# PSUM of the attention stage divided anew in a decoder-layer kernel: logits in two single banks, turned weights in two 1024-column places

## The reference, cut to what matters

```python
score = jnp.where(admissible[None], score, -jnp.inf)
_, idx = lax.top_k(score, topk)                       # 256 keys of each query
logits = jnp.einsum('btngd,btknd->btngk', qg, k_sel) * (HEAD_DIM ** -0.5)
logits = logits + bias                                # T5 bias by distance
p = jax.nn.softmax(logits, axis=-1)
o = jnp.einsum('btngk,btknd->btngd', p, v_sel)
...
y = causal_depthwise_conv(u, conv_w) + conv_b         # width 31
yn = (y - mean(y)) * lax.rsqrt(var(y) + LN_EPS)       # over channels
```

## Time and profile before

| | |
|---|---|
| median of 3 runs | 1701.25 us (1700.36 to 1712.43) |
| span of the profiled execution | 1700.2 us |
| PE matmul busy | 1513.3 us (89%) |
| PE weight load busy | 1292.1 us (76%) |
| DVE busy | 1003.3 us (59%) |
| ACT busy | 697.9 us (41%) |
| POOL busy | 415.0 us (24%) |

### The profile page before, as it was taken

How to read it: one execution, slowest core, us unless ns; L and a number is a source line. 1 busy time by engine, 2 the same in 40 slices (tenths; PEclk the granted TensorE clock), 3 DMA queues, 4 the chain that set the end, 5 groups by cost and what they waited for, 6 DMA issues and landing times. The chain is left out here.

```text
span 1700.2 us, 28238 instructions
## 1 busy us (share of the span) xinstructions
PE 1513.3 (89%) x10647; PEld 1292.1 (76%) x10647; DVE 1003.3 (59%) x2123; ACT 697.9 (41%) x1238; POOL 415.0 (24%) x270
## 2 busy tenths in 40 slices
PE   5688989989998789999799999999999887569998
PEld 5686979978998769999577777776767665348886
DVE  3342998878988879888443444445455555333222
ACT  4354513253112352232225545556556654344331
POOL 2111224431115803222221001112222233043220
PEclk9999999999999999999879999999999999779999
DMA  7742365221357602224561513511111112295542
GB/s 237 219 107 50 68 92 119 67 75 54 84 161 222 157 22 72 70 75 125 163 156 36 115 37 79 113 35 34 39 45 50 58 61 77 81 231 162 173 149 93
DMA packets 183355, 172.71 MB, mean 102 GB/s; under 512 B 58956, under 2 KB 155348, under 8 KB 182700
## 3 DMA queue, kind: packets, MB, share of 16 engines
q1 hardware_dynamic: 176572, 152.91, 33.7%
q10 hardware_dynamic: 6136, 16.95, 3.4%
q0 software_dynamic: 512, 1.05, 0.2%
HBM read 109.35 MB, written 58.19 MB: 99 GB/s over the span
## 5 line engine op out<-in xcount | busy, mean ns | idle before, releaser
L845 PE MATMUL psum<-xh,wh 128*128 128x384 f32 (+1 forms) x1040 | 345.4, 332 | 23.1 <-ACT hst L782 11.5
L845 PE MATMUL psum<-xl,wh 128*128 128x384 f32 (+1 forms) x1040 | 341.6, 329 | 0.0
L845 PE MATMUL psum<-xh,wl 128*128 128x384 f32 (+1 forms) x1040 | 341.6, 328 | 0.0
L1436 ACT ACTIVATE pts<-psT 128x512 f32<-128x512 f32 (+1 forms) x302 | 167.1, 572 | 255.1 <-PE psT L1717 232.2
L845 PEld LDWEIGHTS psum<-xh,wh 128*128 128x128 f32 x1040 | 197.6, 190 | 26.4 <-ACT hst L782 15.2
L1606 DVE CUSTOM_DVE_ANT_0 L<-psU,mask 128x512 f32<-128x512 f32 (+3 forms) x260 | 143.5, 592 | 114.6 <-PE psU L1711 113.3
L1733 PE MATMUL psO<-pts,vs 128*64 128x128 f32 x2176 | 180.3, 287 | 27.2 <-ACT pts L1436 27.2
L845 PEld LDWEIGHTS psum<-xl,wh 128*128 128x128 f32 x1040 | 197.8, 190 | 0.0
L845 PEld LDWEIGHTS psum<-xh,wl 128*128 128x128 f32 x1040 | 197.5, 190 | 0.0
L995 DVE TENSOR_SCALAR_CACHE_REDUCE hit<-scores,T 128x1792 bf16<-128x1792 f32 (+8 forms) x120 | 184.6, 1538 | 11.7 <-issue 0.9
L693 POOL TENSOR_TENSOR wl<-uw,wh 128x1024 fp32r<-128x1024 f32 x44 | 121.5, 2762 | 276.8 <-ACT wh L730 276.8
(11 more groups left out here) (269 smaller groups left out, 2507.5 us busy)
## 6 DMA issues: line engine op xcount, KB each, us to landing
uw<-in_w_in SPq DMA_DIRECT2D x28, 512.0 KB
uw<-in_w_in SPq DMA_DIRECT2D x32, 256.0 KB
qt<-d_q SPq DMA_DIRECT2D x16, 512.0 KB, 4.0
xst<-in_x_prompt SPq DMA_DIRECT2D x15, 512.0 KB, 4.0
xr<-in_x_prompt SPq DMA_DIRECT2D x15, 512.0 KB, 4.4
out_y_prompt<-fin SPq DMA_DIRECT2D x15, 512.0 KB, 3.0
gate<-d_ga SPq DMA_DIRECT2D x17, 256.0 KB, 4.4
d_mix<-mix SPq DMA_DIRECT2D x17, 256.0 KB, 2.2
```

Source lines behind the costliest of these rows:

```text
L845: last = nc.tensor.matmul(u[:, 0:k * P], a[:, w % 2, cc, :], x[:, s0:s0 + k, cc, :], start=(cc == 0 and e == 0), stop=(cc == KC - 1 and e ...
L1436: A.activation(out, src, ACT.Copy).then_inc(act_pt, 1)
```

## The change: what it does, and the diff

PSUM is divided anew: `U` has two single banks (PE may be two pieces ahead of DVE, not four), `PT` has two places of 1024 columns, which are two banks each, and `OT` stays. A group has up to four key blocks of both sides (step 0: eight), made as even as can be by `groups`. ACT copies a group of up to 1024 columns with one instruction. `pts` goes from three places of 512 to two of 1024.

PE's order in a step changes: the next step's pieces are laid between the turns, two by two. A turn waits for the exponentials of its own side alone. ACT takes the next step's first exponential after the first copy where a step has more than two groups, the second after all copies; the copy of the spread reciprocals (`rb`) moves behind both. SBUF buffer `L` loses its pad of 128 columns a row; row 0 alone runs over, for step 0.

```diff
-    per = lambda p: 2 if p else 4
-    groups = lambda p: [(b, min(per(p), nblk(pairs[p][0]) - b)) for b in range(0, nblk(pairs[p][0]), per(p))]
+    per = lambda p: 4 if p else 8
+    def groups(p):
+        n = nblk(pairs[p][0])
+        g = -(-n // per(p))
+        ends = [-(-n * e // g) for e in range(g + 1)]
+        return [(b, e - b) for b, e in zip(ends, ends[1:])]
+    u_pieces = lambda p: [(side, a, k) for side in range(sides(p)) for a, k in bank_pieces(pairs[p][0])]
...
-        pts = sb("pts", [128, 3, 4 * P])
+        pts = sb("pts", [128, 2, 8 * P])
...
-        U = ctx.enter_context(nc.psum_tensor("psU", [128, 2, UNIT], f32))
-        PT = ctx.enter_context(nc.psum_tensor("psT", [128, 2, 512], f32))
+        U = ctx.enter_context(nc.psum_tensor("psU", [128, 2, 512], f32))
+        PT = ctx.enter_context(nc.psum_tensor("psT", [128, 2, 8 * P], f32))
...
-            exps(0)
+            exps(0, 0)
             for p, (i, j) in enumerate(pairs):
-                for b, k in groups(p):
+                for e, (b, k) in enumerate(groups(p)):
                     job = ("T", p, b, k)
                     n = t_no[job]
-                    act.wait_ge(pe_pv, NS + 1 + max(0, n - 2))
+                    act.wait_ge(pe_pv, NS + 1 + max(0, n - 1))
                     m = sides(p) * k * P
-                    evac(job, pts[:, n % 3, 0:m], PT[:, pt_no[job] % 2, 0:m])
+                    evac(job, pts[:, n % 2, 0:m], PT[:, pt_no[job] % 2, 0:m])
+                    if e == 0 and len(groups(p)) > 2 and p + 1 < NP_:
+                        exps(p + 1, 0)
+                if p + 1 < NP_:
+                    if len(groups(p)) <= 2:
+                        exps(p + 1, 0)
+                    exps(p + 1, 1)
...
-                    evac(("R", p), rb[:, n % 2].rearrange("p c t -> p (c t)"), PT[:, pt_no["R", p] % 2, :])
-                if p + 1 < NP_:
-                    if j == GRP - 1 and tile_no[i] >= 1:
-                        act.wait_ge(ri_ready, tile_no[i])
-                    exps(p + 1)
+                    evac(("R", p), rb[:, n % 2].rearrange("p c t -> p (c t)"), PT[:, pt_no["R", p] % 2, 0:4 * P])
...
-                    pe.wait_ge(dve_u, max(first_logits, n - 3))
+                    pe.wait_ge(dve_u, max(first_logits, n - 1))
...
             def transposes(p, b, k):
                 pt = take_pt(("T", p, b, k))
                 for side in range(sides(p)):
+                    if b == 0:
+                        pe.wait_ge(exp_done, sides_before(p) + side + 1)
...
             for p, (i, j) in enumerate(pairs):
-                if p + 1 < NP_:
-                    logits(p + 1)
-                pe.wait_ge(exp_done, sides_before(p + 1))
+                gs = groups(p)
+                more = len(u_pieces(p + 1)) if p + 1 < NP_ else 0
+                if more:
+                    logits(p + 1, 0, 2)
+                transposes(p, *gs[0])
+                if more > 2:
+                    logits(p + 1, 2, 4)
+                if len(gs) > 1:
+                    transposes(p, *gs[1])
+                if more > 4:
+                    logits(p + 1, 4, 6)
...
-                gs = groups(p)
-                transposes(p, *gs[0])
                 for e, g in enumerate(gs):
-                    if e + 1 < len(gs):
-                        transposes(p, *gs[e + 1])
                     products(p, *g)
+                    if e == 0 and more > 6:
+                        logits(p + 1, 6, more)
+                    if e + 2 < len(gs):
+                        transposes(p, *gs[e + 2])
```

More of the change, by code:

```diff
@@ L1454, in _, with exps @@
             evac(("sP", 0), sown[:, :], PT[0:NS, pt_no["sP", 0] % 2, 0:NS * NH])
[L1456 removed]
+            def exps(p, side):
                 i, j = pairs[p]
[L1458 to L1463 removed]
+                n = tile_no[i]
+                if p == first_step(n) and side == 0 and n >= 2:
+                    act.wait_ge(ri_ready, n - 1)
+                act.wait_ge(nm_ready, sides_before(p) + side + 1)
+                b = (2 * p + side) % 4
+                A.activation(Lrow(b, 0, width(i)), Lrow(b, 0, width(i)), ACT.Exp, bias=nm[:, b:b + 1],
+                             accum_out=es[:, n % 2, j % GRP + 4 * side:j % GRP + 4 * side + 1]).then_inc(exp_done, 1)
+            exps(0, 0)
             for p, (i, j) in enumerate(pairs):
[L1465 removed]
+                for e, (b, k) in enumerate(groups(p)):
                     job = ("T", p, b, k)
                     n = t_no[job]
[L1468 removed]
+                    act.wait_ge(pe_pv, NS + 1 + max(0, n - 1))
                     m = sides(p) * k * P
[L1470 removed]
+                    evac(job, pts[:, n % 2, 0:m], PT[:, pt_no[job] % 2, 0:m])
[5 more added lines that the diff above has]
+                    exps(p + 1, 1)
                 if p and j == GRP - 1:
@@ L1677, in _ @@
                 pe.wait_ge(act_pt, act_copies(("page", b)))
[L1678 removed]
+                T.matmul(S[0:NS * NH, 0:PAST], qp[:, b, :], key_part(b), start=(b == 0), stop=False).then_inc(pe_pv, 1)
                 if b + 2 < NS:
@@ L1691, in _, with logits @@
             T.matmul(S[0:NS * NH, PAST:LS], rr, bc[:, PAST:LS], start=False, stop=True).then_inc(pe_u, 1)
-            def logits(p):
+            def logits(p, first, end):
                 i, j = pairs[p]
                 s = tile_no[i] % 2
-                if p == first_step(tile_no[i]):
+                if p == first_step(tile_no[i]) and first == 0:
                     pe.wait_ge(q_in[s], q_loaded(tile_no[i]))
@@ L1705, in logits @@
                     return
-                for side in range(2):
+                for side, a, k in u_pieces(p)[first:end]:
                     q = qt[:, s, j + 4 * side, :]
-                    for a, k in bank_pieces(i):
-                        u = take_u(("L", p, side, a, k))
-                        T.matmul(u[:, 0:k], q, kh[:, side, a:a + k], start=True, stop=False)
-                        T.matmul(u[:, 0:k], q, kl[:, side, a:a + k], start=False, stop=True).then_inc(pe_u, 1)
+                    u = take_u(("L", p, side, a, k))
+                    T.matmul(u[:, 0:k], q, kh[:, side, a:a + k], start=True, stop=False)
+                    T.matmul(u[:, 0:k], q, kl[:, side, a:a + k], start=False, stop=True).then_inc(pe_u, 1)
             def transposes(p, b, k):
@@ L1764, in turn @@
                 last.then_inc(pe_pt, 1)
-            logits(0)
+            logits(0, 0, len(u_pieces(0)))
             pe.wait_ge(s_norm, 1)
```

44 lines of the change are left out of this document (19 added, 25 removed).

## The result

| | before | changed |
|---|---|---|
| median of the runs, us | 1702.2 (4 runs, 1700.36 to 1712.43) | 1690.67 (4 runs, 1686.43 to 1695.35) |
| ratio of the medians, 95% interval | | 0.9919 [0.9891, 0.9946] |
| span of the profiled execution, us | 1700.2 | 1693.7 |
| mean granted clock of TensorE | 0.960 | 0.941 |

The change makes the kernel faster by 0.8% (0.5 to 1.1%), less than the bound of 1% that the prediction used for faster. 1682 was forecast, 1665 to 1706 the range. The profiled execution of the changed kernel is the slowest of its four (1695.35), so the two traces differ by 6.5 us where the medians differ by 11.5.

What follows compares the result with a forecast made beforehand. PE was taken to bound the wide steps, a chain through POOL and DVE the narrower tiles. The terms -35 - 6 + 9 + 11 + 2 gave -19 us: 1682 us against 1701.25, forecast 1674 to 1694, range 1665 to 1706.

Steps and rivals of the forecast that it cites:

- The chain: Tiles 10 to 4: VectorE's multiply waits for POOL, its mask and load; PE waits 4.5 to 9 us in third steps.
- tiles 10 to 8: The chain with waits of 4.5 to 5.5 us each: 116 us against 121.8, -6 us before the clock's charge.
- up to step 1: Step 0 and the logits of tile 16 gain and lose half a microsecond: 0.
- tiles 15 to 11: Wide steps: fewer changes of shape at 0.17 us each, -35 us; bounds from nothing to 40.
- tiles 7 to 4: The chain makes PE wait, 7 us in tile 7: 126 us against 117.4, +9 us before the clock's charge.
- tiles 3 to 0: Tile 3's single group leaves its copy of 1.03 us bare, `rb` lets PE turn earlier: +2 us.
- The waits for the convolution's add: Ten steps where DVE first adds the convolution's bias: PE waits sooner with two banks, 0.3 us each.
- The clock: Half clock behind the new waits in tiles 10 to 4: 1.6 us each, +11 us, bounds 0 and 16.
- The `rb` copy: In tiles 1 and 0, the copy behind the exponentials lets PE turn 0.6 us earlier once a tile.
- The second rival: The chain doesn't bind, POOL getting the mask earlier or the third piece finding a bank: about 1637 us; chance 0.07.
- The third rival: The exponential between first and second copy delays 32 steps with three or more groups: 1724 at 1.3 us each; chance 0.10.
- The fourth rival: PE's clock falls in the wide steps, a tenth of their 245 us at half clock: 25 us, 1707; chance 0.07.

Runs made afterwards that it cites:

- e1: The changed kernel with POOL taking the inverse deviation ahead of the band mask; 1625.33 us, ratio 0.9539 to the kernel before.
- e9: The kernel before with the deviation first on POOL and the `rb` copy behind the next step's exponentials; 1674.44 us, ratio 0.9837.
- e8: e3 with four single logits banks for two and turned places of 512 columns; 1660.67 us, ratio 0.9758 to the kernel before.
- e6: e1 with both exponentials of the next step behind all of the step's copies; 1634.74 us, ratio 0.9598 to the kernel before.
- e10: e8 with POOL's order as it was, mask and band ahead of the deviation; 1715.8 us, ratio 1.0069 to the kernel before.
- e3: e1 with groups of two key blocks again (four in the first step) and four places for copies; 1682.03 us, ratio 0.9863.
- e7: e1 with groups of two key blocks in tiles 3 to 0; 1622.49 us, ratio 0.9526 to the kernel before.
- e4: The kernel before with its logits in two banks of the four, all else as before; 1786.47 us, ratio 1.0484.

## Why the prediction was nearly right

The chain came as forecast and the time lies in the range; of the stretches, only tiles 10 to 8 came out with the other sign. On whether the gain can be told, the forecast leaned the wrong way: it gave 0.56 to a gain of over 1% and 0.37 to none that it could tell, and the gain is 0.8%.

| stretch | forecast | measured |
|---|---|---|
| up to step 1 | 0 | +3.5 |
| tiles 15 to 11 | -35 | -29.8 |
| tiles 10 to 8 (-6, and 3 x 1.6 of clock) | -1.2 | +3.5 |
| tiles 7 to 4 (+9, and 4 x 1.6 of clock) | +15.4 | +15.5 |
| tiles 3 to 0 | +2 | +0.8 |
| sum | -19 | -6.5 |

- **The mechanism was right**: the chain binds in the third steps of tiles 10 to 4, at the third piece of logits, with the clock at 0.50 behind the wait. Forecast was a wait of 7 us in tile 7 and a tile of 34.2, or 35.8 with the clock; measured 5.86 and 35.18. e1 shows the cause by taking it away. That tiles 7 to 4 agree within 0.1 us is in part luck: without the clock they came out 1 us shorter than the sum, and the clock cost 8.1 us there, not 6.4.
- **The step that was mis-sized is the wide one.** Forecast plain steps of 11.7, 11.0, 10.4, 9.7 and 9.0 us; measured 12.10, 11.20, 10.70, 10.51 and 9.25. The 0.17 us a change is right, in these rows of the changed kernel's step 2 too:
```profile
905.02 0.85 PEld L1748 LDWEIGHTS psO<-pts,vs 128*64 128x64 f32 x16 [0.37 <-issue]
...
906.04 0.19 PEld L1721 LDWEIGHTS psU<-keys,qt 128*128 128x128 f32 x1 [0.17 <-DVE mx L1620]
...
908.06 0.85 PEld L1748 LDWEIGHTS psO<-pts,vs 128*64 128x64 f32 x16 [0.17 <-issue]
909.09 0.85 PEld L1732 LDWEIGHTS psT<-cst,L 128*128 128x128 f32 x8 [0.17 <-issue]
910.11 0.85 PEld L1748 LDWEIGHTS psO<-pts,vs 128*64 128x64 f32 x16 [0.17 <-issue]
911.36 0.85 PEld L1748 LDWEIGHTS psO<-pts,vs 128*64 128x64 f32 x16 [0.39 <-ACT pts L1447]
```
  What stayed is the last products' wait for ACT's copy, 0.39 us here and in the plain steps of tiles 15, 12 and 11 (0.2 in those of tiles 14 and 13), which I had at 0.1 to 0.2, and 0.37 ahead of the first products, where I had 0.17. Tile 12 gained 1.17 where I had 2.0, the largest miss; my sum had its four groups already, and what took the rest of it isn't shown. The waits for the convolution's add (3 us) did not come: its steps gained like the plain ones.
- **The sign to look for was badly chosen.** I said that 24.8 us of "issue" waits at the products would fall by more than half; they are 24.1. Of tiles 15 to 11 alone, the three rows of turns and products (`psO` for ACT, `psO` and `psT` for issue) add up to 49.3 us before and 22.9 after, with 3.3 more before for `psT` behind ACT: -29.7, close to the stretch's -29.8 (the logits' waits for VectorE fell by another 4.0, 11.6 to 7.6, so the agreement is partly chance). A change of shape that ends with ACT's copy is counted under ACT, so these rows must be read together.
- **The clock** was put at 11 us (0 to 16) and is 15.4 by e1's rows, near the upper bound: 1.6 to 3.0 us a step. It fell on other work than I took the 1.6 us from. The turns of the result in tiles 9 to 5 take 2.05 us, as at the full clock in the earlier trace rows; what runs at 0.50 is the work right behind the wait, the logits and turns first.
- **Tiles 10 to 8** were taken with done tiles and chains guessed from tile 7's. The waits were right: 4.2, 4.3 and 5.2 us at the third piece, where 4.5 to 5.5 were forecast. What was too small is the rest: the three tiles without waits, about 101 us in my sum (116 less some 15 of waits), take 104.7 in e1, and the clock cost 7.3 us, not 4.8. So the steps themselves and the clock were mis-sized here, not the chain.
- **The `rb` copy** was charged with 0.6 us a tile and is worth about 1.3 (e9). In tiles 10 to 4 that gain can't be seen in the changed kernel by itself; a step that starts sooner may wait longer for the same chain, which no run separates.
- **Up to step 1** I see no cause in the change: the 14 traces have step 1 begin anywhere between 883.1 (e8) and 893.3 us, and e1, whose instructions differ from the changed kernel's only from step 22 on, begins it at 884.2 where the changed kernel has 888.1.
- **The second rival** (no chain, 1637) had a chance of 0.07 as a forecast of this kernel, and rightly so; but it is what the kernel is worth with one loop's order turned round (1625.33). I had judged that nothing in the written order would free it, and didn't ask what it would cost to write it otherwise.
- **The third rival** was wrong of the wide steps (e6) and right of the third ones (e10): in e10 the exponential waited 5.06 us and held the copy behind it for that long, while in tiles 15 to 11 of the changed kernel its waits are short (20 of them, 14.8 us, at most 1.1).
- **The rule on breaking up instructions** (the Trainium skill, Perfetto Trace Analysis, Optimizing Scalar/DVE Operations) would have made the steps slower, +28 us over 64 steps by the prediction's sum; the wide ones are 29.8 faster, and e3, which breaks the copies up again, is 57 us slower. (It breaks up TensorE's groups along with them, so it doesn't price the copies alone.) It holds where a tile has one group alone and nothing covers the copy: e7, 3.1 us in tiles 3 and 2.
- **The fourth rival** did not come: the windows of the plain steps show a clock of 1.00.

## What to carry to other kernels

Before buffers are taken from a queue between two engines, look for the longest stall of the consumer that they cover now, however rare, and follow it back to its cause; here the cause was the order of two independent jobs on POOL, free to turn round, and that was worth more than five times the change. Fewer, larger groups pay by the changes that they save and by the waits that stood behind each change, so price them with an experiment rather than with the bare gap. And an in-order engine should do first the job that someone waits for, and last the one whose input or reader is steps away.

## What the runs showed that I had not expected

- Behind a wait of 5.86 us TensorE ran at a granted clock of 0.50 for some 4 us: eight turns took 1.91 us for 1.04. In the seven third steps this made 27% more busy time for the same matmuls (71.9 us for 56.5), 15.4 of the 57.2 us lost.
- A change between turns (128*128) and products (128*64) costs an idle of 0.17 us, but 0.20 to 0.27 us a change of step time (e3).
- POOL's power of 128x8 values takes 1.65 us, where its multiply and add on the same tile takes 0.20; it is the last link before VectorE in the chain.
- Taking two of four banks costs 37.5 us in the wide steps with the logits in one row (e4), and 7.2 with the pieces spread (e3 less e8); neither says what it costs in a third step.
